# Adding the bias of the compressed attention branch on TensorE, by a product with the unit matrix, and not on VectorE

## What is computed

```python
s = jnp.einsum('btgrd,bngd->btgrn', q, kc) * scale
dist = q_pos[:, None] - c_end[None, :]
bias = table[rel_bucket(dist)].transpose(0, 2, 3, 1)[None]
p_c = masked_softmax(s + bias, (dist >= 0)[None, :, None, None, :])
o_cmp = jnp.einsum('btgrn,bngd->btgrd', p_c, vc)
```

## Time and profile before

| what | value |
|---|---|
| median of three runs | 1118.57 us (1116.58 to 1119.76) |
| profiled execution | 1115.21 us |
| its span, first to last instruction | 1113.2 us, 22587 instructions |
| TensorE, matmul busy | 1075.2 us, 97% of the span |
| TensorE, weight loads busy | 763.3 us, 69% |
| VectorE | 624.6 us, 56% |
| ScalarE | 362.5 us, 33% |
| GpSimd | 86.5 us, 8% |
| mean granted TensorE clock | 0.991 of full speed (2.4 GHz) |

### The profile page before, as it was taken

The page is one execution under the profiler, slowest core; times in us unless marked ns, Lnnn a source line. Parts: engine busy times, 40 slices in busy tenths (PEclk is TensorE's granted clock), DMA queues, the critical chain, the costliest instruction groups (busy, mean ns, idle before and its releaser), DMA issues. The chain is left out here.

```text
span 1113.2 us, 22587 instructions
## 1 busy us (share of the span) xinstructions
PE 1075.2 (97%) x8368; PEld 763.3 (69%) x8368; DVE 624.6 (56%) x1627; ACT 362.5 (33%) x893; POOL 86.5 (8%) x184
## 2 busy tenths in 40 slices
PE   6899999999999999998999999999999999999997
PEld 3455599998886677776776657664544576777775
DVE  0645323463423477769677766742323588888883
ACT  0322001121112475546555555631112133333330
POOL 0210100110000011101101010011000200000000
PEclk9899999999999999999999999999999999999998
DMA  9933270001006240000000000005794467878781
GB/s 355 310 115 94 72 211 2 16 19 72 1 1 122 44 116 2 1 1 2 1 2 1 2 1 2 1 1 119 169 307 152 142 217 262 271 274 275 261 251 51
DMA packets 96612, 120.25 MB, mean 108 GB/s; under 512 B 31569, under 2 KB 65380, under 8 KB 95480
## 3 DMA queue, kind: packets, MB, share of 16 engines
q1 hardware_dynamic: 96504, 118.81, 34.4%
HBM read 104.41 MB, written 14.36 MB: 107 GB/s over the span
## 5 line engine op out<-in xcount | busy, mean ns | idle before, releaser
L549 PE MATMUL PS<-AR 128*128 128x256 f32 (+2 forms) x896 | 219.7, 403 | 0.0
L549 PEld LDWEIGHTS PS<-AR 128*128 128x128 f32 x896 | 167.8, 190 | 45.2 <-issue 6.2
L2090 PE MATMUL PS<-AR 128*128 128x512 f32 x256 | 112.3, 592 | 0.0
L1747 PE MATMUL PS<-CA,AR 128*128 128x128 f32 x704 | 111.4, 282 | 0.8 <-ACT AR L1821 0.8
L963 DVE TENSOR_TENSOR AR<-PS,AR 128x256 f32<-128x256 f32 (+2 forms) x80 | 36.2, 452 | 134.4 <-PE PS L549 134.3
L1747 PEld LDWEIGHTS PS<-CA,AR 128*128 128x128 f32 x704 | 77.0, 143 | 44.6 <-issue 31.7
L1821 ACT ACTIVATE AR<-PS 128x512 f32<-128x512 f32 (+1 forms) x108 | 58.2, 546 | 125.1 <-PE PS L1747 124.5
L1725 PE MATMUL PS<-AR 128*128 128x65 f32 (+1 forms) x688 | 89.3, 271 | 0.0
L2090 PEld LDWEIGHTS PS<-AR 128*128 128x128 f32 x256 | 47.5, 190 | 54.0 <-issue 54.0
L1725 PEld LDWEIGHTS PS<-AR 128*128 128x128 f32 x688 | 84.3, 192 | 0.0
L1806 ACT ACTIVATE AR<-PS,SM_ 128x512 f32<-128x512 f32 (+4 forms) x192 | 76.6, 471 | 15.9 <-DVE SM_ L1914 8.8
(11 more groups left out here) (364 smaller groups left out, 1622.9 us busy)
## 6 DMA issues: line engine op xcount, KB each, us to landing
AR<-in_cache_nsa SPq DMA_DIRECT2D x128, 256.0 KB, 5.0
AR<-in_cache_mla SPq DMA_DIRECT2D x128, 96.0 KB, 3.7
AR<-in_x_prompt SPq DMA_DIRECT2D x16, 512.0 KB, 4.6
AR<-in_w_ada SPq DMA_DIRECT2D x3, 2048.0 KB, 11.4
AR<-in_w_in SPq DMA_DIRECT2D x6, 1024.0 KB, 8.4
AR<-in_w_ada SPq DMA_DIRECT2D x8, 512.0 KB, 4.3
AR<-in_w_out SPq DMA_DIRECT2D x4, 1024.0 KB, 10.0
AR<-in_w_out SPq DMA_DIRECT2D x2, 2048.0 KB, 17.5
```

What stands on the lines that cost most here:

```text
L549: mm = pe.matmul(bank[:, 0:WIDE[g]], tokens[:, k, :], w, start=(fresh and k == 0), stop=(last and k == 3), skip_group_check=True)
L1747: mm = pe.transpose(PS[:, 4 + c % 2, P * (t - t0):P * (t - t0) + P], tile(u, t), ident)
L2090: mm = pe.matmul(PS[0:n, 2 + 2 * (m % 2) + c, :], YTO[m % 2][:, f, 0:n], weights[:, f, 512 * c:512 * c + 512], start=(f == 0), stop=(f == 7))
```

## The change

After each of the two score products of a `cmp` unit TensorE makes a second product into the same 128 columns of PSUM, accumulating: the unit matrix as the stationary operand and the unit's columns of `BCX` as the moving one. VectorE's addition and its wait for it are gone; the minimum reads the sum from PSUM. The wait for `BCX` (`s_btw`) moves from VectorE to TensorE.

```diff
--- before.py
+++ after.py
@@ -1674,8 +1674,12 @@
             elif before >= 0:
                 pe.wait_ge(s_exp, EXP0[before] + 2 if split or MANY[before] and not TWO[before] else EXP0[before + 1])
             if kind == "cmp":
+                if i == 0:
+                    pe.wait_ge(s_btw, 6)
                 for n in range(2):
-                    mm = pe.matmul(scores(u, 2 * n, 0, P), QT[:, 2 * half + n, q], KCX, start=True, stop=True)
+                    pe.matmul(scores(u, 2 * n, 0, P), QT[:, 2 * half + n, q], KCX, start=True, stop=False)
+                    mm = pe.matmul(scores(u, 2 * n, 0, P), ident, BCX[:, 2 * half + n, :, 56 - 8 * i:120 - 8 * i],
+                                   start=False, stop=True)
                 mm.then_inc(s_qk, 1)
                 return
             runs = key_runs(kind, i, k0, nb)
@@ -1893,13 +1897,6 @@
                         dve.wait_ge(s_mx, far_count[0])
                 dve.wait_ge(s_qk, QK0[u + 1])
                 if kind == "cmp":
-                    if i == 0:
-                        dve.wait_ge(s_btw, 6)
-                    s = scores(u, 0, 0, 256).rearrange("p (r g c) -> p r g c", r=2, g=G)
-                    dve.tensor_tensor(s, s, BCX[:, 2 * half:2 * half + 2, :, 56 - 8 * i:120 - 8 * i], ALU.add)\
-                        .then_inc(s_mx, 1)
-                    far_count[0] += 1
-                    dve.wait_ge(s_mx, far_count[0])
                     ins = dve.tensor_reduce(nm, scores(u, 0, 0, 256).rearrange("p (h c) -> p h c", h=4), AX, ALU.min)
                     if i == 0:
                         ins.then_inc(s_mx, 1)
```

## The result

Over 22 runs of each kernel, the three shown ahead among those of before, the changed kernel has a median of 1116.64 us (1113.80 to 1123.05), the kernel before 1114.19 (1110.57 to 1119.76, and one run of 3079 us, without which the median is 1114.02). The ratio, without that run, is **1.0034, 95% interval 1.0019 to 1.0049**, which is 3.8 us, between 2.1 and 5.5; the two means without it lie 3.83 us apart, the two medians by themselves 2.45. The forecast was slower by 4.1 us, at 1122.7 us: the interval of the difference holds the 4.1, and it lies across the 0.3% that can be told from no change; the time is 6 us under the forecast and under the whole range.

The account below looks back on a forecast made before the run. TensorE bounds the dense units, VectorE the packed stretch; -0.1 (first tile) + 2.65 (dense) + 1.6 (packed) = +4.1 us on the median 1118.57 gives 1122.7 us, range 1119.3 to 1125.6.

Parts of the forecast that it names:

- The price: On TensorE, each added f32 product is two records of 0.11 us: 0.22 a product, 0.44 a unit, 7.0 for sixteen.
- Rival 2: Compressed units: added products run at half price like transposes, one record, 0.22 us a unit; +0.7 us, 1119.3; chance 0.10.
- rival 1: Compressed units: product cheap, 0.085 us or less, VectorE's relief wins; not slower, at best 2.4 us gained (1116.2); chance 0.07.
- First tile -0.1: First query tile, two units: 0.88 us of products fits TensorE's wait before the latent scores, which ends earlier; -0.1 us.
- dense units +2.65: Second to fourth query tile, six units where TensorE is dense: each pays 0.44 us in full, +2.65 us.
- Packed stretch +1.6: Eight units, 499.5 to 514.4 us: 3.54 of work less 1.50 of gaps and 0.40 of refills; step 1.55; +1.6 us.
- Rival 3: Packed stretch: a longer path to the next scores keeps TensorE's gaps, nothing is absorbed; +7.0 us, 1125.6; chance 0.09.
- Behind it only a shift: After the packed stretch: TensorE's 1.95 us wait before 521.29 gives no cover; later stages start later, lengths unchanged.
- The formula: Whole change at price a per unit, up to 0.17 us: 6a dense, -0.45 first tile, 8a - 1.9 packed; 14a - 2.4 us.
- The point of no change, 0.17: Whole change: nothing comes out at 0.17 us a unit, that is 0.085 us a product.
- the 1.9 us of the packed stretch: Packed stretch: 1.50 us of gaps and 0.40 of refills go, subtracted from the eight units' added work.
- the step from the profiled execution to the runs: Whole kernel: the +4.1 us sum, 1119.3 from the profiled execution, was put on the runs' median 1118.57, giving 1122.7.

Follow-up runs that it names:

- before, third: The kernel before, unedited, traced a third time: execution 1110.79 us, 127.07 us from the first compressed scores to the window scores behind the packed stretch.
- bf16: Against the changed kernel, bias table and unit matrix in bf16 in all units: stretch 127.16 us, ratio 1.0013 to the kernel before.
- two bf16: Against the changed kernel, two bf16 products per score product, rounded bias and rounding remainder: stretch 128.85 us, ratio 1.0013 to the kernel before.
- a price of nothing: Against the changed kernel, no unit product and no VectorE addition, scores without bias and mask: stretch 125.03 us, ratio 0.9988 to the kernel before.
- the kernel that did gain there: Against the changed kernel, bf16 product only in first tile and packed stretch, VectorE adding in tiles 1 to 3: stretch 126.16 us, ratio 0.9997.
- before, again: The kernel before, unedited, traced a second time: execution 1112.24 us, 127.49 us from the first compressed scores to the window scores behind the packed stretch.

## Why the prediction was right and where it was wrong

**The price, right.** 0.22 us a product, two records of 0.11, taken from a dense group of ordinary scores: measured 0.44 us a unit in all six dense units, 0.445 with the product doubled. No surcharge for the strided bias shows. Rival 2 (one record, as a transpose) falls with the rows of line 1681, two records to a product. The busy share of the weight loads over the span is 69% after as before, and every added record of a dense unit was paid all the same: by the stretches there was no room. The Trainium skill's rule weighed in rival 1 (Trainium Kernel Development and Optimization, Performance Expectations), taken over the whole span, would have found some room.

**First tile -0.1, dense units +2.65, right.** Step by step, the dense units of the trace after grew by 0.44 to 0.45 six times, and the first tile by 0.44 - 0.48 - 0.06 = -0.10. The kernel with these parts alone gave +2.64, corrected for its clock, for a sum of +2.55.

**Packed stretch +1.6, right.** Alone it gave +1.72; the waits before the scores are gone; the step is 1.56 for 1.55 forecast. Rival 3 falls: VectorE's finishing (515.35, its end) is through 0.15 us before the minimum at 515.50 and holds nothing up.

**Behind it only a shift, right.** The wait is 1.91 for 1.95, and the next stage is 231.76 us in before, third, and 231.76 and 231.77 in the two later traces of after.

**The formula, right in shape.** The changes of the stretch against the price of a unit (the prediction gives the formula up to a price of 0.17; the third row goes beyond that):

| price of a unit, us | measured | 14a - 2.4 |
|---|---|---|
| 0 | -2.04 | -2.4 |
| 0.16 (bf16) | +0.09 | -0.2 |
| 0.28 (two bf16) | +1.78 | +1.5 |
| 0.44 (f32) | +4.32 | its sum: +4.1 |

The point of no change, 0.17, is 0.02 too high: at 0.16 the stretch has grown by 0.09 already, and 14 us for each us of price put it at 0.154. The term that was too large is the 1.9 us of the packed stretch at a price of nothing, which measured 1.54: I let TensorE's work set its step (1.11), and the trace has 1.22 to 1.25, with VectorE and ScalarE both nearly full. The prediction's own row spoke against 1.11: it has ScalarE busy 1.3 us a step (4.98 of 6.30 us in some four steps). The f32 case does not hang on that term, since TensorE sets its step; its +0.2 is for the most part the packed stretch, 1.72 for 1.6. Against the first trace of before, with its chance loss of 0.19, the change reads +4.11.

**The time, wrong: the step from the profiled execution to the runs.** "The median of the runs, 1118.57, lies 3.4 us above the profiled one, and I put the same sum on it": that step failed. Three runs were taken for the kernel's level. Over 22 runs its median is 1114.19, so these three lay 4.4 us high, by chance as far as is known; the sum of 4.1 on 1114.19 makes 1118.3, already under the range, and 1116.64 was measured. The profiled execution, 1115.21, was the nearer guide, and the text had 1119.3 from it. The range had a term for each price and none for the level, though single traces of one kernel differ by 4.5 us of span (1113.2 and 1108.7), 3.1 of them through the granted clock near the end. The medians lie 2.45 us apart, against 4.32 in the stretch; the means lie 3.83 apart, and the interval of the ratio, 2.1 to 5.5 us, holds them all. The median says less here, because the runs of after stand in two groups: fourteen from 1113.80 to 1117.52 us with a mean granted clock of 0.990 to 0.994, and eight from 1119.28 to 1123.05 us with 0.984 to 0.987. I have no trace of the second group, so in which stage its clock is lower stays open.

## What to carry to other kernels

Adding a bias by a product with the unit matrix pays only where TensorE waits for the engine that is relieved: weigh the added records' pace (here 0.44 us a unit) against the idle time stretch by stretch, and do it only in the units where idle time covers it. Idle time alone does not: at 0.44 us a unit the packed stretch lost 1.7 us for all its gaps, and the kernel that did gain there (0.91 us, with bf16) cannot be told from no change in its runs. When a change is worth a few microseconds, compare the lengths between the same two events in both traces, not spans, and give the level of the runs a term of its own in the range; three runs do not fix it to 0.4%.

## What the runs showed of the hardware that was not expected

A bf16 product between f32 ones is not paid by its own record alone: 0.06 us for the record, and 0.06 more on the pair of f32 score records behind it (0.28 against 0.22). A second bf16 product right behind the first brought only its own 0.06 (0.28 - 0.16 = 0.12 a unit of two), and the transposes behind a bf16 product take 0.44 us (485.30 to 485.74) as they do before (446.49 to 446.93). Why the score pair pays and the transposes do not was not found.

The granted clock falls to half, 1.2 GHz, at places that change from execution to execution of one kernel (the traces are not all of the same chip): around 390 us with a loss of 0.95 us in one, right behind 525 us with 0.37, around 760 us with 1.7, at 885 to 889 us with 1.65, from 1094 us with 3.1. Ahead of four of these places TensorE had stood still (1.22 us before 385.15, 1.91 us before 524.34, 0.88 us before 759.35, 2.73 us before 885.06); ahead of the last, in the first trace of before, it was busy for all of 1080 to 1094 us. And it stood still 2.72 us ahead of 886.79 in before, again, too, and there it had 1.00. So standing still ahead of it is not enough, nor is it always there, and what decides was not found.
